# The down projection of ten tile pairs as seven block products, in a fused float32 decoder trunk

## What is computed

```python
def conv_glu_ffn(h, w_up, conv_w, w_down):
    gu = h @ w_up
    g, u = jnp.split(gu, 2, axis=-1)
    g = causal_dwconv(g, conv_w)
    return (jax.nn.silu(g) * u) @ w_down

def reference(x, positions, ...):
    h = x
    for layer in range(DEPTH):
        hn = rms_norm(h, norm_mix_g[layer])
        h = h + hybrid_mixer(hn, positions, ...)
        hn = rms_norm(h, norm_ffn_g[layer])
        h = h + conv_glu_ffn(hn, w_up[layer], conv_ffn_w[layer], w_down[layer])
    return rms_norm(h, final_g)
```

## Time and profile before

| | |
|---|---|
| Time, median of 3 runs | 2489.36 us (2486.4 to 2489.61) |
| Span of the profiled execution | 2486.1 us |
| PE busy | 2410.3 us, 97% |
| DVE busy | 1499.8 us, 60% |
| POOL busy | 1190.9 us, 48% |
| ACT busy | 893.7 us, 36% |

### The profile page before, as it was taken

One profiled execution on the slowest core, in us unless ns is written; L12 is line 12 of the kernel. 1 busy time (PEld: TensorE's weight loads), 2 busy tenths in 40 slices (PEclk: granted clock), 3 DMA queues, 4 the chain that ended last, 5 costly groups with the idle time before them and its releaser, 6 DMA issues.

```text
span 2486.1 us, 31278 instructions
## 1 busy us (share of the span) xinstructions
PE 2410.3 (97%) x11580; PEld 2002.5 (81%) x11580; DVE 1499.8 (60%) x2161; ACT 893.7 (36%) x1716; POOL 1190.9 (48%) x777
## 2 busy tenths in 40 slices
PE   7999999999999999999999999999999999999998
PEld 6888888777888888888778888878778888888886
DVE  8654777648555555555695556784575555555555
ACT  4344444425323233223424344453342322222333
POOL 3121122447666666666431211241676666666665
PEclk9999999999999999999999999999999999999999
DMA  3100101221111111111220010112221111111111
GB/s 139 35 26 26 35 27 50 90 66 35 52 51 51 52 57 63 52 51 51 97 86 26 26 35 26 32 58 59 60 68 51 51 52 51 51 51 51 52 51 68
DMA packets 55751, 131.37 MB, mean 53 GB/s; under 512 B 4784, under 2 KB 24368, under 8 KB 55600
## 3 DMA queue, kind: packets, MB, share of 16 engines
q1 hardware_dynamic: 54016, 128.07, 15.6%
q10 hardware_dynamic: 1584, 1.28, 0.2%
HBM read 119.64 MB, written 9.44 MB: 52 GB/s over the span
## 4 chain that ended last, share of the span: by engine, by line
PE 74%; DVE 16%; ACT 4%; issue 3%; POOL 1%; DMA 1%; DVEq 0%; SPq 0%; POOLq 0%; ACTq 0%
PE ps L855 14%; PE ps L856 14%; PE ps L857 14%; PE ps L826 7%; PE ps L828 7%; PE ps L827 7%; PE ps L1134 4%; DVE k_next L2106 3%; PE ps L1121 2%; DVE h L1754 1%; PE ps L1108 1%; PE ps L1109 1%; DVE padded L2078 1%; DVE k_next L2113 1%; ACT prob L1494 1%
## 5 line engine op out<-in xcount | busy, mean ns | idle before, releaser
L599 POOL CAST w_hi<-stage 128x1024 fp32r<-128x1024 f32 x68 | 73.3, 1078 | 782.5 <-PE ps L828 710.2
L634 POOL TENSOR_TENSOR w_lo<-more_stage,w_hi 128x512 fp32r<-128x512 f32 x204 | 300.9, 1475 | 216.4 <-ACT w_hi L1569 198.6
L826 PE MATMUL ps<-x_hi,w_hi 128*128 128x512 f32 x928 | 374.4, 403 | 7.5 <-DVE q_next L1662 4.6
L634 POOL TENSOR_TENSOR w_lo<-stage,w_hi 128x512 fp32r<-128x512 f32 x186 | 268.9, 1446 | 202.6 <-ACT w_hi L1569 184.7
L828 PE MATMUL ps<-x_hi,w_lo 128*128 128x512 f32 x928 | 364.1, 392 | 0.0
L827 PE MATMUL ps<-x_lo,w_hi 128*128 128x512 f32 x928 | 362.9, 391 | 0.0
L1682 DVE TENSOR_TENSOR h<-ps,h 128x1024 f32<-128x1024 f32 x160 | 194.1, 1224 | 192.5 <-PE ps L857 189.6
L855 PE MATMUL ps<-mix,w_hi 128*128 128x512 f32 x708 | 280.4, 396 | 9.8 <-DVE h L1682 7.5
L856 PE MATMUL ps<-mix,w_hi 128*128 128x512 f32 x708 | 277.3, 392 | 0.0
L857 PE MATMUL ps<-mix,w_lo 128*128 128x512 f32 x708 | 276.7, 391 | 0.0
L855 PE MATMUL ps<-T_hi,w_hi 128*128 128x512 f32 x688 | 269.7, 392 | 6.8 <-DVE q_next L2078 5.4
(11 more groups left out here) (243 smaller groups left out, 4631.9 us busy)
## 6 DMA issues: line engine op xcount, KB each, us to landing
stage<-stream SPq DMA_DIRECT2D x112, 512.0 KB, 3.8
more_stage<-stream SPq DMA_DIRECT2D x68, 512.0 KB, 4.4
h<-x_t SPq DMA_DIRECT2D x16, 512.0 KB, 7.0
stage<-stream SPq DMA_DIRECT2D x18, 448.0 KB, 4.7
saved_h<-h SPq DMA_DIRECT2D x8, 512.0 KB, 5.8
h<-saved_h SPq DMA_DIRECT2D x8, 512.0 KB, 3.3
out_t<-h SPq DMA_DIRECT2D x16, 256.0 KB, 2.5
stage<-stream SPq DMA_DIRECT2D x18, 64.0 KB, 5.2
```

The source lines that it names most:

```text
L634: pool.tensor_tensor(block_of(w_lo, n), raw, block_of(w_hi, n).bitcast(f32), ALU.subtract)\
L826: pe.matmul(out, w_hi[:, s, w], hi, start=start, stop=False)
```

## The change

For the first ten pairs of each layer the down product becomes a block product of its own: weights of the pair as 2 x 2 blocks (128 of the 256 hidden features by 512 of the 1024 outputs), the value as 2 x 2 blocks (tile by half of the positions), seven products of 4 rows of 3 matmuls instead of eight. Part A (products B11 and T1) runs ahead of the even up tile, part B (T2, B21, T3, B22, T4) behind it. The sums T1 to T4 of the value are made by VectorE (`form`), rounded by ScalarE, and their rests are taken by VectorE. Products of the banks 4 to 7 (CHAINED) go on adding on top of what stands in the bank, so that VectorE adds the running sum to more than one part of `h`; the other four rows use the banks 0, 1, 3, 2 (SINGLE), which the up tiles use too, and so up tiles wait for adds to `h`. GpSimd makes the four sums of the pair's weight blocks, and its order inside `weights` changes. The split weights take three block places instead of four in the steady part (W_RING), as the fourth place holds T4's halves. The semaphore for free slots becomes one for each slot, up tiles use the slots 1 and 0, down tiles 2 and 3. `value` moves on VectorE from the end of an up tile to behind the adds of the part that follows. The last pair stays as it was.

```diff
-ADDS = (PAIRS - 1) * KT + 2 * KT
+ROWS = KT // 2
+PART_A_DOWNS, PART_B_DOWNS = 2 * ROWS, 5 * ROWS
+PART_A_ADDS, PART_B_ADDS = 3 * ROWS, 5 * ROWS
+PAIR_DOWNS, PAIR_ADDS = PART_A_DOWNS + PART_B_DOWNS, PART_A_ADDS + PART_B_ADDS
+DOWNS = (PAIRS - 1) * PAIR_DOWNS + 2 * KT
+ADDS = (PAIRS - 1) * PAIR_ADDS + 2 * KT
...
+W_RING = (1, 2, 3)
...
-SLOT_ORDER = (2, 3, 1, 0)
+UP_SLOTS, DOWN_SLOTS = (1, 0), (2, 3)
...
-        work += [("up", 2 * pair + 2), ("down", pair), ("up", 2 * pair + 3)]
+        work += [("part_a", pair), ("up", 2 * pair + 2), ("part_b", pair), ("up", 2 * pair + 3)]
...
+def block_places():
+
+    count, whole = len(weight_blocks()), 2 * PRODUCTS
+    place = [(n + 2) % W_BLOCKS for n in range(whole)]
+    place += [W_RING[n % len(W_RING)] for n in range(count - whole - W_BLOCKS)] + list(range(W_BLOCKS))
+    before = [n - W_BLOCKS for n in range(whole)]
+    before += [n - len(W_RING) for n in range(whole, count - W_BLOCKS)]
+    before += [count - W_BLOCKS - PRODUCTS - 1] + [n - W_BLOCKS for n in range(count - W_BLOCKS + 1, count)]
+    return place, before
...
-        DOWN = SCORE + 2
+        CHAINED, SINGLE = (4, 5, 6, 7), (0, 1, 3, 2)
+        UP_ADDED = (5, 6, 6, 7)
...
+                s1, s2, s3, s4 = a21, a11, a22, a21
...
                 combine(s1, a21, a22, ALU.add)
                 pool.sem_inc(block_raw, 1)
-                combine(s3, a11, a21, ALU.subtract)
+                rest_of_block(a11)
                 combine(s2, s1, a11, ALU.subtract)
-                pool.sem_inc(block_raw, 3)
+                pool.sem_inc(block_raw, 1)
+                rest_of_block(a22)
+                combine(s3, a22, s2, ALU.subtract)
+                pool.sem_inc(block_raw, 2)
                 rest_of_block(s1)
+                combine(s4, a12, s2, ALU.subtract)
+                pool.sem_inc(block_raw, 1)
                 rest_of_block(s2)
                 rest_of_block(s3)
                 rest_of_block(a12)
+                rest_of_block(s4)
+                for s in UP_SLOTS:
+                    pool.sem_inc(stage_free[s], 1)
+
...
+            def first_down_weights():
+
+                (a11, a21), (a12, a22) = staged(), staged()
+                s1, s2 = a21, a11
+                pool.sem_inc(block_raw, 1)
+                combine(s1, a21, a22, ALU.add)
+                pool.sem_inc(block_raw, 1)
+                rest_of_block(a11)
+                combine(s2, s1, a11, ALU.subtract)
+                rest_of_block(s1)
+                return s2, s1, a12, a22
+
+            def second_down_weights(s2, s3, a12, a22):
+                s4 = s2
+                pool.sem_inc(block_raw, 2)
+                combine(s3, a22, s2, ALU.subtract)
+                pool.sem_inc(block_raw, 1)
+                rest_of_block(s2)
                 combine(s4, a12, s2, ALU.subtract)
-                pool.sem_inc(block_raw, 1)
+                pool.sem_inc(block_raw, 2)
+                rest_of_block(a12)
+                rest_of_block(s3)
                 rest_of_block(s4)
-                pool.sem_inc(stage_free, 2)
-
-            def down_weights():
+                rest_of_block(a22)
...
+                    elif f % 2 == 0:
+                        pe.wait_ge(add_done, added + ROWS + 2 * (SINGLE.index(b) + 1))
+                    else:
+                        pe.wait_ge(add_done, added + PART_A_ADDS + 3 * ROWS + SINGLE.index(b) + 1)
...
+            def down_row(n, x, m, b, start):
+
+                columns = slice(m * P, (m + 1) * P)
+                hi, lo = mixed_halves[x]
+                pe.matmul(bank(b), block_of(w_hi, n)[:, columns], hi, start=start, stop=False, skip_group_check=True)
+                pe.matmul(bank(b), block_of(w_hi, n)[:, columns], lo, start=False, stop=False, skip_group_check=True)
+                pe.matmul(bank(b), block_of(w_lo, n)[:, columns], hi, start=False, stop=True, skip_group_check=True)\
+                  .then_inc(down_done, 1)
+
+            def part_a(layer, pair):
+                added, formed = layer * ADDS + pair * PAIR_ADDS, 2 * (layer * (PAIRS - 1) + pair)
+                a11, s1 = next_block(), next_block()
+                pe.wait_ge(block_ready, a11 + 1)
+                pe.wait_ge(first_formed, formed + 1)
+                for m, b in enumerate(CHAINED):
+                    if pair:
+                        pe.wait_ge(add_done, added - ROWS + m + 1)
+                    down_row(a11, "B11", m, b, True)
+                pe.wait_ge(block_ready, s1 + 1)
+                pe.wait_ge(first_formed, formed + 2)
+                for m, b in enumerate(SINGLE):
+                    pe.wait_ge(combined, PRODUCTS * (layer * F_TILES + 2 * pair + 1) + UP_ADDED[m])
+                    down_row(s1, "T1", m, b, True)
+
+            def part_b(layer, pair):
+                added = layer * ADDS + pair * PAIR_ADDS
+                here, formed = added + PART_A_ADDS, 4 * (layer * (PAIRS - 1) + pair)
+                s2, a12, s3, s4, a22 = (next_block() for _ in range(5))
+                pe.wait_ge(block_ready, s2 + 1)
+                pe.wait_ge(second_formed, formed + 4)
+                for m, b in enumerate(CHAINED):
+                    pe.wait_ge(add_done, added + m + 1)
+                    down_row(s2, "T2", m, b, False)
+                pe.wait_ge(block_ready, a12 + 1)
+                for m, b in enumerate(SINGLE):
+                    pe.wait_ge(combined, PRODUCTS * (layer * F_TILES + 2 * pair + 2) + UP_ADDED[m])
+                    down_row(a12, "B21", m, b, True)
+                pe.wait_ge(block_ready, s3 + 1)
+                for m, b in enumerate(CHAINED):
+                    pe.wait_ge(add_done, here + m + 1)
+                    down_row(s3, "T3", m, b, False)
+                pe.wait_ge(block_ready, s4 + 1)
+                for m, b in enumerate(SINGLE):
+                    pe.wait_ge(add_done, here + ROWS + m + 1)
+                    down_row(s4, "B22", m, b, True)
+                pe.wait_ge(block_ready, a22 + 1)
+                for m, b in enumerate(CHAINED):
+                    pe.wait_ge(add_done, here + 2 * ROWS + m + 1)
+                    down_row(a22, "T4", m, b, False)
...
+            def keep_first_value():
+                act.wait_ge(value_ready, seen(value_ready))
+                act.activation(mixed_halves["B11"][0], k_next[:, 0:HALF], ACT.Copy).then_inc(hi_ready, 1)
+                act.activation(mixed_raw["B12"], k_next[:, HALF:], ACT.Copy).then_inc(hi_ready, 1)
+
+            def round_formed(*names):
+                for x in names:
+                    act.wait_ge(formed_raw, seen(formed_raw))
+                    act.activation(mixed_halves[x][0], mixed_raw[x], ACT.Copy).then_inc(hi_ready, 1)
...
+            def add_part_a():
+                add_rows(CHAINED, (0, 0))
+                add_rows(SINGLE, (ROWS, 1), (0, 1))
+
+            def add_part_b():
+                add_rows(CHAINED, (0, 1))
+                add_rows(SINGLE, (0, 0))
+                add_rows(CHAINED, (ROWS, 1))
+                add_rows(SINGLE, (0, 1))
+                add_rows(CHAINED, (ROWS, 0))
...
+            def form(x, a, b):
+                dve.tensor_tensor(mixed_raw[x], a, b, ALU.subtract).then_inc(formed_raw, 1)
+
+            def rest_formed(x, done):
+                dve.wait_ge(hi_ready, seen(hi_ready))
+                hi, lo = mixed_halves[x]
+                dve.tensor_tensor(lo, mixed_raw[x], hi.bitcast(f32), ALU.subtract).then_inc(done, 1)
+
+            def first_of_pair():
+
+                form("T1", k_next[:, HALF:], k_next[:, 0:HALF])
+                dve.wait_ge(formed_raw, seen(formed_raw))
+                dve.wait_ge(hi_ready, seen(hi_ready))
+                hi, lo = mixed_halves["B11"]
+                dve.tensor_tensor(lo, k_next[:, 0:HALF], hi.bitcast(f32), ALU.subtract).then_inc(first_formed, 1)
+                dve.wait_ge(hi_ready, seen(hi_ready))
+                rest_formed("T1", first_formed)
+
+            def second_of_pair(layer, pair):
+
+                dve.wait_ge(first_formed, 2 * (layer * (PAIRS - 1) + pair + 1))
+                form("T2", k_next[:, HALF:], mixed_raw["T1"])
+                form("T3", k_next[:, HALF:], mixed_raw["B12"])
+                dve.wait_ge(formed_raw, seen(formed_raw, 2))
+                form("T4", k_next[:, 0:HALF], mixed_raw["T2"])
+                dve.wait_ge(formed_raw, seen(formed_raw))
+                dve.wait_ge(hi_ready, seen(hi_ready))
+                dve.tensor_tensor(mix_lo[0], k_next[:, :], mix_hi[0].bitcast(f32), ALU.subtract).then_inc(second_formed, 1)
+                for x in ("T2", "T3", "T4"):
+                    rest_formed(x, second_formed)
 
...
                             combine(layer, n)
-                    elif n < PAIRS - 1:
-                        for m in range(KT):
-                            add_down(m)
-                        value_rest(2 * n + 2)
+                    elif what == "part_a":
+                        add_part_a()
```

(13 more changed lines are left out.)

225 lines of the change are left out of this document (125 added, 100 removed).

## The result

The changed kernel takes 2584.44 us, the median of 4 runs (2581.11 to 2586.49), against 2489.22 of the kernel before beside it (4 runs, 2486.4 to 2489.61): the ratio is 1.0384, with a 95% interval of 1.0371 to 1.0397. It is slower by 95 us. The profiled execution has a span of 2584.5 us, 98.4 above that of before.

What follows compares the result with a forecast made beforehand. TensorE's matmul stream was taken as the bound. A pair: 57.13 + 1.7 + 3.4 + 1.7 = 63.93 against 60.18, +75 us for 20 pairs; first pairs +9; 2486.1 + 84 = 2570, plus 3.3 for the median: 2573 us, range 2494 to 2610.

Steps and rivals of the forecast that it cites:

- Slots, waits, engines beside: Steady pair: 252 matmul slots, 57.13 us; satisfied waits, ScalarE and SP at nothing; GpSimd 48.5 us undisturbed.
- the fifth rival: TensorE saves no slots because start=False rows or 512-column waits cost more; no chance of its own, folded into upper end.
- rival 3: GpSimd becomes the bound of a steady pair, 59.5 to 63.9 us, middle 61.7: 2529 us; chance 0.09.
- The stalls: TensorE waits 1.7 us behind part A for an add, then 3.4 at the even tile's sixth product for the first combination.
- The contention: VectorE's 512-column SBUF operations behind part A wait for GpSimd: 1.64 us for five, 0.69 for one.
- The clock: TensorE's clock falls to half behind the 3.4 us stall, 1.7 us a pair; nothing charged behind the 1.7 us stall.
- the fourth rival: The first stall of each pair takes the clock down as well, 34 us more: 2607 us; chance 0.09.
- The first pairs: First pair of each layer, in addition: +0.9, +3.1, +1.7 and -1.0, so 4.7 us a layer, +9 in all.
- The old wait: First pair of a layer: TensorE's existing 2.71 us wait for combinations, lengthened by 0.9 through three operations replacing one.
- The first stall of 4.8: First pair of each layer: the wait behind part A is 4.8 us (+3.1) and takes the clock down (+1.7).
- The first rival: Added VectorE SBUF operations are cheap, 1.13 us each, and the clock is kept: 2497 us; chance 0.18.
- the second 0.91: Rival: VectorE hides the nine added operations, under 0.91 us each, so no second stall: 2471 us, faster; chance 0.12.

Runs made afterwards that it cites:

- e2: The changed kernel with GpSimd's combinations and low parts of weight blocks in steady pairs cut to 128 of 512 columns (work left out): 2438.29 us, ratio 0.9796.
- e11: e8 with part A's twelve adds in mixed order, so that bank 0 is free after three instead of six: 2488.49 us, ratio 1.0000 to the kernel before.
- e12: The changed kernel with T2's, T3's and T4's low parts moved behind the first combination and part A's adds in mixed order: 2462.99 us, ratio 0.9899.
- e5: The changed kernel with 18 matmuls of zero weights filling the second stall of each pair: 2555.45 us, ratio 1.0267 to the kernel before.
- e4: The changed kernel with the low parts of T2, T3 and T4 formed by GpSimd instead of VectorE: 2520.18 us, ratio 1.0130 to the kernel before.
- e3: The changed kernel with one more 512-column VectorE subtraction, result unused, between the forms of T2 and T3: 2591.75 us, ratio 1.0413 to the kernel before.
- e1: The changed kernel without the low parts of T2, T3 and T4 (matmuls kept, result incomplete): 2462.57 us, ratio 0.9894 to the kernel before.
- e8: The changed kernel with T3's low part moved behind the tile's last combination, T4's behind part B's first four adds: 2487.77 us, ratio 1.0000.

## Why the prediction came out as it did

The forecast of 2573 lies 11 us below the measured 2584, and the mechanism (slower, by VectorE's queue and then the clock) is what the runs showed. That it came so near is in part luck. The pairs added 93 us and not 75, the first pairs 5 and not 9, and the 3.3 added for the median being above the profiled span was nothing here (2584.44 against 2584.5): 18 - 4 - 3.3 is the 11. Step by step:

**Slots, waits, engines beside.** 252 matmuls a pair, and e2's 57.18 us shows that slots, the many satisfied waits and rows added on top of a bank cost nothing beyond 57.13. That is the fifth rival's end. SP and ScalarE cost nothing visible. GpSimd was busy 49.4 us; the predicted 48.5 can't be set beside that, since it includes a gap of 0.18 for each operation. Undisturbed, 33 x 1.29 is 42.6, so 6.8 are VectorE's disturbance, and with the gaps GpSimd is occupied for 55.3 of 64.65 us. It isn't the bound (1.4 us of waits for its blocks in all the up tiles), and rival 3's 59.5 was too high; but e11 and e12 show that it had no room behind the first stall, nearer than the prediction had it.

**The stalls.** Counted from the start of part A, 814.89, as I did it; measured against predicted:

| | predicted | measured |
|---|---|---|
| last combination of the odd tile ends | 2.74 | 2.86 (817.75) |
| next product starts, behind the sixth add | 7.15 | 6.50 (821.39) |
| twelve adds end | 11.44 | 9.95 (824.84) |
| value, with the turn to the next | 1.61 | 1.95 |
| six forms and low parts, with gaps | 9.2 | 10.05 (5.0 and 5.05) |
| rest of 1024 columns | 1.22 | 2.12 |
| first combination starts | 23.5 | 24.07 (838.96) |
| sixth product starts | 24.2 | 24.80 (839.69) |

Without stalls TensorE would start the sixth product after 5.44 + 13.6 = 19.04; both stalls together are 5.8 us against 5.1. The split was off: the first is 1.1 rather than 1.7, the second 4.7 rather than 3.4. Four terms were mis-sized. The adds came at 0.60 us each instead of 0.725, because I had taken the spacing of combinations that wait for each other, and adds don't (-1.5). The rest of 1024 columns I priced from a row in which GpSimd did not disturb it; here it took 2.20 (+0.9). The forms took 1.55 to 1.78 and no one of the six came at 0.69, as the prediction had it for one without a row (+0.8). The value took 0.3 more. By luck the errors nearly cancel, +0.6 us in 24. Adding the stalls as two losses was right in the sum only because the end of one queue sets both; e11 shows that speeding up the first gives nothing by itself.

**The contention.** 1.64 was near the truth: the ones that stand back to back show 1.55 to 1.78. The Trainium skill, page "SBUF — State Buffer", section "Who interferes with whom", lets the later of two wait fully; an estimate by that rule is up to 0.69 + 1.29 = 1.98. The rule's kind is borne out by e2 (0.69), its upper end is not reached.

**The clock.** Predicted 1.7 us a pair behind the second stall, none behind the first; measured 1.65 (e5), and 1.00 granted behind the first. This also ends the fourth rival. Of the waits read here, those of 0.9 us and of 2.16 (e4) left the clock full, one of 1.9 and one of 2.6 did so in the change and not in e3, and those of 4.3 in the steady pairs lowered it, so the length of a wait alone doesn't say what the clock does. By the Trainium skill, page "TensorE: Matmul & The Clock Gate", section "A second HAM failure mode: psum-queue depth-cycling", frequent short idling makes the clock go to and fro; here 0.9 us once or twice a pair did not (e1, e8).

**A pair.** 57.13 + 1.1 + 4.7 + 1.65 = 64.6 of the measured 64.85, against 63.93 predicted. The starts in the two pairs shown above place the rest: beside the stalls (5.75 and 5.70) and the matmuls at half clock (1.57 and 1.60), many starts are a few hundredths of a us late, 0.2 together in the first of the pairs and 0.5 in the second.

**The first pairs.** Predicted 4.7 a layer, some 9 in all; about 5 remained. VectorE and TensorE there:

```profile
606.90 1.64 DVE L1860 TENSOR_TENSOR mix<-k_next,mix 128x512 fp32r<-128x512 f32 x1
608.46 1.75 DVE L1852 TENSOR_TENSOR mix<-mix_raw,mix 128x512 fp32r<-128x512 f32 x1
```

```profile
611.59 0.79 PE L937 MATMUL ps<-T_hi,w_hi 128*128 128x512 f32 x1 [5.53 <-DVE q_next L2262]
621.05 0.50 PE L1015 MATMUL ps<-mix,w_hi 128*128 128x512 f32 x1 [1.91 <-POOLq L684]
625.90 0.50 PE L937 MATMUL ps<-B_hi,w_hi 128*128 128x512 f32 x1 [0.36 <-DVE h L1819]
```

The old wait of 2.71 grew to 5.53 and not to 3.6: two of the three new operations met GpSimd, 1.64 and 1.75 instead of 0.69. The first stall of 4.8 did not come; because TensorE is itself late, and waits 1.91 us for GpSimd inside part A, 0.36 was left of it. This step failed in its parts; two errors of opposite sign made a small one.

**The chances.** The first rival (cheap operations) needed 1.13 us, the second 0.91; of the six none was under 1.55 in the steady pairs shown. The first rival's own row, eight rests at a median of 1.13, came from operations spaced by others; these stand back to back. That reading carried the forecast. A spaced one in the changed kernel bears it out: T1's low part behind a pause of 0.71 us, beside a GpSimd that had only its gaps of 0.18:

```profile
867.47 0.98 DVE L1852 TENSOR_TENSOR mix<-mix_raw,mix 128x512 fp32r<-128x512 f32 x1 [0.71 <-ACT mix L1714]
```

## What to carry to other kernels

Before adding work to an engine that isn't the bound, write down its queue between two points where the bounding engine waits for it, with each operation at its price beside its neighbour: 24 us of added work fit into VectorE's pair, and cost 95 us mainly because six of the new operations stood ahead of one of 0.7 us that TensorE needed. Ask of each operation who needs its result and when; moving three of them behind the one that was awaited, with no operation saved, took 2584 to 2465. (VectorE's busy time fell with it, from 56.1 to 54.1 us a pair, as the moved ones took less.) Two waits ahead of the same queue's end are one debt: speeding up the earlier one moves the wait, and taking the work to GpSimd, which was nearly full, made a wait there. Count an engine's gaps with its busy time before you call it idle.

## What was not expected of the hardware

Adds of one PSUM bank each to SBUF, 0.68 us long in the profile, follow each other every 0.60 us when none waits for another (12 in 7.25 us, beside a busy GpSimd); combinations that wait for each other came every 0.725. And the price of an SBUF operation of VectorE is elastic: the same 512-column subtraction for a low part took 0.68, 1.06 and 1.77 us within one pair of e8, by how it met GpSimd's, so that one more of them left the length of the queue where it was (e3).
